# A two-block transformer: the scan's causal mask moves from TensorE products to a 0/1 triangle on the C-B factor

## What is computed

```python
a_cs = jnp.cumsum(a_c, axis=-1)
decay = jnp.exp(segsum(a_c))        # exp(cs[t] - cs[s]) for s <= t, else 0
cb = jnp.einsum("bclgn,bcsgn->bgcls", cm_c, bm_c)
y_diag = jnp.einsum("bgcls,bgrcls,bcsgrp->bclgrp", cb, decay, xs_c)
```

## Time and profile before

| | |
|---|---|
| median of 3 runs | 1653.1 us (1649.43, 1653.1, 1655.61) |
| profiled execution | 1655.45 us, span 1653.8 us |
| PE busy | 1593.0 us, 96% |
| PEld busy | 1541.0 us, 93% |
| POOL busy | 1271.9 us, 77% |
| DVE busy | 925.4 us, 56% |
| ACT busy | 866.3 us, 52% |
| mean DMA rate | 183 GB/s |

### The profile page before, as it was taken

How to read it: one execution, slowest core, us unless ns; L and a number is a source line. 1 busy time by engine, 2 the same in 40 slices (tenths; PEclk the granted TensorE clock), 3 DMA queues, 4 the chain that set the end, 5 groups by cost and what they waited for, 6 DMA issues and landing times.

```text
span 1653.8 us, 33845 instructions
## 1 busy us (share of the span) xinstructions
PE 1593.0 (96%) x13182; PEld 1541.0 (93%) x13182; DVE 925.4 (56%) x1799; ACT 866.3 (52%) x1432; POOL 1271.9 (77%) x948
## 2 busy tenths in 40 slices
PE   7999999999999999999999899999999999999999
PEld 6999988898999999999998899999999998799999
DVE  7767777567646763467677757754442256632200
ACT  3554555554456663465455564545664455655532
POOL 1878967675779999678986767697998786279996
PEclk7999999999999999999999999999999999999999
DMA  8545744446446657455764545654665664146654
GB/s 306 178 146 204 244 165 160 142 166 242 166 141 235 235 200 255 149 156 174 242 207 144 164 155 192 231 178 148 184 190 174 200 202 142 47 152 192 183 188 128
DMA packets 85518, 302.23 MB, mean 183 GB/s; under 512 B 9840, under 2 KB 12528, under 8 KB 85104
## 3 DMA queue, kind: packets, MB, share of 16 engines
q1 hardware_dynamic: 85360, 300.06, 55.3%
HBM read 298.98 MB, written 1.05 MB: 181 GB/s over the span
## 4 chain that ended last, share of the span: by engine, by line
PE 71%; DVE 11%; ACT 5%; DVEq 4%; issue 3%; POOL 2%; DMA 2%; SPq 1%; ACTq 0%; POOLq 0%
PE gemm_bank L1688 63%; ACT w_hi L443 2%; POOL w_lo L425 2%; PE turn_bank L1871 2%; PE turn_bank L1842 2%; DVEq L1337 2%; DVE ada_acc L848 1%; DVE conv L848 1%; DVE h_lo L1383 1%; DVE idx_score L848 1%; DMA ada_first<-in_w_ada 1%; DVE probs L1045 1%; DVEq L1221 1%; PE outp_bank L2078 1%; PE score_bank L1688 1%
## 5 line engine op out<-in xcount | busy, mean ns | idle before, releaser
L425 POOL TENSOR_TENSOR w_lo<-w_raw,w_hi 128x512 fp32r<-128x512 f32 x944 | 1271.7, 1377 | 370.7 <-ACT w_hi L443 357.8
L443 ACT ACTIVATE w_hi<-w_raw 128x1024 fp32r<-128x1024 f32 x472 | 491.7, 1046 | 590.6 <-PE gemm_bank L1688 517.5
L1688 PE MATMUL gemm_bank<-h_hi,w_hi 128*128 128x256 f32 (+1 forms) x2144 | 608.8, 284 | 7.2 <-DVE conv L848 3.7
L1688 PE MATMUL gemm_bank<-h_hi,w_lo 128*128 128x256 f32 (+1 forms) x2144 | 601.2, 280 | 0.0
L1688 PE MATMUL gemm_bank<-h_lo,w_hi 128*128 128x256 f32 (+1 forms) x2144 | 600.8, 280 | 0.0
L1688 PEld LDWEIGHTS gemm_bank<-h_hi,w_hi 128*128 128x128 f32 (+1 forms) x2144 | 403.9, 188 | 16.2 <-issue 7.4
L1688 PEld LDWEIGHTS gemm_bank<-h_lo,w_hi 128*128 128x128 f32 (+1 forms) x2144 | 404.5, 189 | 0.3
L1688 PEld LDWEIGHTS gemm_bank<-h_hi,w_lo 128*128 128x128 f32 (+1 forms) x2144 | 404.0, 188 | 0.2
L848 DVE SCALAR_TENSOR_TENSOR conv<-gemm_bank,params_sb,conv 128x255 f32<-128x255 f32 (+1 forms) x320 | 139.5, 477 | 161.9 <-ACT conv L774 110.7
L1688 PE MATMUL gemm_bank<-w_hi,h_hi 128*128 128x256 f32 (+1 forms) x672 | 193.5, 288 | 2.7 <-DVE h_lo L848 1.5
L1688 PE MATMUL gemm_bank<-w_lo,h_hi 128*128 128x256 f32 (+1 forms) x672 | 188.0, 280 | 0.0
(11 more groups left out here) (310 smaller groups left out, 2165.2 us busy)
## 6 DMA issues: line engine op xcount, KB each, us to landing
w_raw<-in_stream SPq DMA_DIRECT2D x458, 512.0 KB, 3.8
ada_w<-in_w_ada SPq DMA_DIRECT2D x80, 512.0 KB, 4.6
ada_first<-in_w_ada SPq DMA_DIRECT2D x16, 512.0 KB, 12.1
w_raw<-in_stream SPq DMA_DIRECT2D x8, 256.0 KB, 3.1
alibi_sb<-in_alibi SPq DMA_DIRECT2D x1, 1920.0 KB, 7.8
residual<-in_x_t SPq DMA_DIRECT2D x1, 1024.0 KB, 6.7
ada_acc<-in_rows SPq DMA_DIRECT2D x1, 1024.0 KB, 5.1
out_x<-residual SPq DMA_DIRECT2D x4, 256.0 KB, 4.6
```

The lines of the kernel that those rows point to most:

```text
L425: ins = nc.gpsimd.tensor_tensor(w_lo[:, s, e], w_raw[:, s, e], w_hi[:, s, e].bitcast(f32), ALU.subtract)
L443: A(w_hi[:, s, 0:n], w_raw[:, s, 0:n], ACT.Copy).then_inc(hi_ready, 1)
L1688: ins = M(o, a, b, start=first and i == 0, stop=last and i == len(passes) - 1, skip_group_check=True)
```

## The change

The mask is no longer added on PE. A 0/1 triangle `seen_T` (1 where s <= t), made once in the setup, multiplies the diagonal blocks of `CB` as DVE moves them out of PSUM. Since the exponents above the diagonal are now positive and could overflow, ACT first bounds those of the diagonal blocks: it writes relu(cs[s] - cs[t]) with the new column `pos_cs` as bias, and then takes exp of its negative. The block between them (columns 128 to 255) is exponentiated as before. A drain of ACT stands between the Relus and the Exp that reads them. So a head has four ACT instructions and a drain where it had two, and two PE products where it had four.

```diff
-        ident_b = sb("ident_b", [P, P], bf16)
-        maskT_b = sb("maskT_b", [P, P], bf16)
+        seen_T = sb("seen_T", [P, P], bf16)
+        pos_cs = sb("pos_cs", [P, TT, 32])
...
             def decayed_exp(l, h):
                 b, k = S.use(l, S_SSM + h)
                 act.wait_ge(S.full[b], k + 1)
-                A(S.bank[b][:, 0:2 * P], S.bank[b][:, 0:2 * P], ACT.Exp, bias=neg_cs[:, 0, h:h + 1])
-                A(S.bank[b][:, 2 * P:CW], S.bank[b][:, 2 * P:CW], ACT.Exp, bias=neg_cs[:, 1, h:h + 1]).then_inc(decay_done, 1)
+                o = S.bank[b]
+                for c, tt in ((0, 0), (SEQ, 1)):
+                    A(o[:, c:c + P], o[:, c:c + P], ACT.Relu, scale=-1.0, bias=pos_cs[:, tt, h:h + 1])
+                A(o[:, P:SEQ], o[:, P:SEQ], ACT.Exp, bias=neg_cs[:, 0, h:h + 1])
+                act.drain()
+                seen = o[:].rearrange("p (b c) -> p b c", b=2)[:, :, 0:P]
+                A(seen, seen, ACT.Exp, scale=-1.0).then_inc(decay_done, 1)
...
-            V.tensor_copy(ident_b[:], ident)
...
-            V.tensor_copy(maskT_b[:], keep_bias[:, 0:P]).then_inc(set_up, 1)
+            V.tensor_scalar(seen_T[:], keep_bias[:, 0:P], -1.0, None, ALU.is_ge).then_inc(set_up, 1)
...
                 def group_product(g):
                     b, k = S.use(l, S_CB + g)
                     dve.wait_ge(S.full[b], k + 1)
-                    V.tensor_copy(CB[:, g, :], S.bank[b][:, 0:CW]).then_inc(S.read[b], 1)
+                    V.tensor_tensor(CB[:, g, 0:P], S.bank[b][:, 0:P], seen_T[:], ALU.mult)
+                    V.tensor_copy(CB[:, g, P:SEQ], S.bank[b][:, P:SEQ])
+                    V.tensor_tensor(CB[:, g, SEQ:CW], S.bank[b][:, SEQ:CW], seen_T[:], ALU.mult).then_inc(S.read[b], 1)
...
+                        V.tensor_copy(pos_cs[:], T.bank[b][:, 0:64].rearrange("p (t h) -> p t h", t=TT))
                         V.tensor_scalar(neg_cs[:], T.bank[b][:, 0:64].rearrange("p (t h) -> p t h", t=TT), -1.0, None, ALU.mult
...
-                    ins = products([(o[:, 0:SEQ], row, cs_split[:, :]), (o[:, SEQ:CW], row, cs_split[:, P:SEQ]),
-                                    (o[:, 0:P], ident_b[:], maskT_b[:]), (o[:, SEQ:CW], ident_b[:], maskT_b[:])], True, True)
+                    ins = products([(o[:, 0:SEQ], row, cs_split[:, :]), (o[:, SEQ:CW], row, cs_split[:, P:SEQ])], True, True)
```

## The result

The changed kernel takes 1674.35 us (median of 4 runs, 1672.72 to 1677.49), the kernel before on the same chip 1651.26 (4 runs, 1648.99 to 1655.61): ratio on record 1.0123, 95% interval 1.0089 to 1.0156, some 20 us slower (the two medians are 23.1 us apart). The forecast was 1664 us, 11 us slower. The profiled execution took 1677.49 us (span 1675.9), 22.0 more than that of before; the mean granted clock fell from 0.988 to 0.978.

The account below looks back on a forecast made before the run. PE was taken as the bound, 71% of the chain, with ACT and DVE carrying parts of the scans. First layer 5.6 plus second 5.0 made 10.6 us later: profiled 1655.45 to 1666.1, median about 1664, range 1651 to 1674.

Parts of the forecast that it names:

- ScalarE's head: ACT's decay exponentials of one scan head: 0.63 us added to 0.69, bounds 0.45 and 0.80 more.
- No table loads of its own: ACT's Relus in the scan need no table switch; the rival claim was 164 us of loads, chance 1%.
- The three C-B operations: DVE's moves of C-B out of PSUM: three 128-wide take 0.60 us against 0.47, so 0.13 more each time.
- DVE's wait for the exponentials: Sign in the first layer's scan: DVE's wait for ACT grows from 25 to some 36 us.
- The mask products: PE in the scan: a pair is worth 0.13 us; six groups on the chain give back 0.78 a layer.
- rival 1: Scans: PE decides everywhere, ACT's added time hides, mask products are gained: -8.3 + 0.5, 1645 us; chance 8%.
- The second block: Sign: the same stretches stay unchanged in the second block.
- the C-B terms: The C-B factor: two added 0.13 us ahead of PE's wait for the second copy, 0.26 a layer, 0.5 in both.
- The count of heads: Scans: ACT's added time counts 22 times, once for each head whose exponentials are on the chain, less 3.3 us.
- PE's waits for DVE: Sign in the scans: they grow from 7 to about 16 us a layer.
- Rival 3: Scans: longer PE waits cost clock, 1.7 us a fall, two to four more: +3.4 to +6.8, to 1669; chance 13%.
- The bound of 3 us for both layers: Upper limit on the added C-B time, if each 128-wide DVE operation takes 0.42 us.

Follow-up runs that it names:

- experiment 3: Also `pe_only`: kernel before without the mask products on PE, nothing in their place, Tanhs for Exps; 1653.53 us, ratio 0.9999.
- `after_again`: The changed kernel measured once more, unaltered, beside the kernel before; 1673.58 us, ratio 1.0122.
- filler: The changed kernel with unused products on PE ahead of its waits; 1665.3 us, ratio 1.0067.
- `cb_only`: Also experiment 1: kernel before with C-B moved out of PSUM in three 128-wide DVE operations, two masked; mask products and exponentials kept; 1659.71 us, ratio 1.0046.
- `before_delay`: The kernel before with one unused 0.28 us DVE copy ahead of its first C-B copy; 1653.15 us, ratio 1.0007.
- `before_warm`: The kernel before with unused products on PE ahead of its waits; 1656.44 us, ratio 1.0011.
- experiment 9: The same run as `before_delay`: kernel before with one unused 0.28 us DVE copy ahead of its first C-B copy; 1653.15 us, ratio 1.0007.
- number 8: The kernel before with DVE moving C-B out ahead of the top-eight search of the same step; 1648.56 us, ratio 0.9963.
- `after_one_cb`: The changed kernel with C-B moved and masked in one 384-wide DVE operation, using an 8-bit triangle; 1658.02 us, ratio 1.0023.
- `after_all`: The changed kernel with one 384-wide masked C-B operation, C-B ahead of top-eight search, three ScalarE instructions a head and unused PE products; 1657.35 us, ratio 1.0017.

## Why the prediction was right in direction and half in size

**Right.** Direction, and the steps behind it. ScalarE's head: 0.58 us more, for 0.63 forecast. No table loads of its own. The three C-B operations: 0.14 more, for 0.13. DVE's wait for the exponentials: 36.9 us, for "some 36". The mask products: a gain too small to measure, against 8.3 if PE had decided everywhere (experiment 3), so rival 1 is out. The second block lost under 2 us. That 1674.35 lies at the very end of the range, 1674, is luck: that end was worked out with a head of 0.80 more, which measured 0.58, and with two falls of the clock, which were more.

**Right in size, by another route.** The scans were forecast 10.1 us longer (10.6 less the C-B terms); they grew by 8.5 in this run (150.6 + 147.8 against 145.1 + 144.9), by 9.6 in `after_again`. The count of heads was low: the forecast had 22 on the path, the chain of the changed kernel has 26, 13 in each scan. But PE's waits for DVE grew by 4.5 us in the first scan and 4.8 in the second, not by the 9 each that the forecast named. Less the 8.3 us of products that are gone, these waits alone would give 1.0. The clock records of the scans have one fall before and five after, seven in `after_again`; with 1.7 us each that is the rest, 6.8 to 10.2. With filler there was none, and the scans grew by 4.4. That smaller added waits and the falls of the clock together come near the forecast's 10.1 is luck. Waits and clock can't be parted cleanly: a slower PE comes later to its waits and finds them shorter.

**Wrong, the clock.** Rival 3 had the mechanism, its price and 13%, and it was kept as an alternative to the sum. It came on top of it: filler gives back 9 us. This is the term that the sum had at nothing. It was also counted in the scans alone, two to four times 1.7. It came there, in both C-B stages (5.0 us together) and in the second attention, which lost 5.0. In that last place some kernels with the old exponentials have such falls too, in their profiled runs (`cb_only`, `pe_only`, `before_delay`, `before_warm`). In the first attention it is even the other way round, 10.2 us at 1.2 GHz before and 3.4 after. So it is open whether the change is what lowered the clock there.

**Wrong, the C-B factor.** This term of the sum was 0.26 us a layer. It counted the copies ahead of the one that PE waits for, and took every operation between them at its old duration. The running sum stands between them, beside a busy POOL, and grew by 1.1 us because it started on the other side of a POOL instruction (experiments 1 and 9). The measured wait is 1.23 longer a layer, and with the clock the stages lost 8.3 us. The bound of 3 us for both layers was from the C-B operations' own durations, so it didn't hold this. Alone, the C-B part costs 7.6 us (3.6 to 11.6).

**The parts don't add.** Alone they measure +7.6 (C-B), +18.7 (exponentials) and 0 (products), 26 together for 20. The exponentials' part has the widest interval (13 to 24), and the clock and the pace of PE's stream differ from run to run. With the clock loss taken off, the spans are longer than before's by 3 us (C-B), 11 (exponentials) and 9 (all of the change), and 1 shorter (products); the clock loss has grown by 2, 5, 10 and 0. So without the clock the exponentials cost about what their forecast had.

## What to carry to other kernels

Where the profile shows that longer waits of PE cost clock, put that price into the sum instead of keeping it as an alternative, and test it with filler products. Before an instruction is put ahead of others on VectorE, look at which of these run beside a busy GpSimd: a shift of 0.2 us can change another instruction's time by 1 us. Work taken from the busiest engine gains nothing where a chain through two others ends later, and an order change on another of PE's waits (number 8) gained 6 us, where the products on the chain were worth 1.6.

## What the runs showed of the hardware

**The lock between DVE and POOL.** In all 14 profiled runs the running sums of the two layers take either 0.68 us, where they begin 0.06 to 0.09 us ahead of a POOL product (which then takes 1.7), or 1.70 to 1.78, where they begin 0.05 to 0.13 behind its start; nothing lies between. In every such case they end 0.54 us after POOL's product. The second block's running sum does the same: 0.68 in twelve runs, and 1.62 in the two in which it begins 0.21 behind POOL's start, again ending 0.54 after POOL's product.

**Two paces of PE.** At the full clock the 256-column products of a weight stream follow each other in one of two spacings. PE's timeline near the end, the kernel before, then `after_one_cb`:

```profile
1599.75 0.28 PE L1688 MATMUL gemm_bank<-f_lo,w_hi 128*128 128x256 f32 x1
...
1601.16 0.28 PE L1688 MATMUL gemm_bank<-f_lo,w_hi 128*128 128x256 f32 x1
```

```profile
1599.80 0.28 PE L1696 MATMUL gemm_bank<-f_lo,w_hi 128*128 128x256 f32 x1
...
1601.16 0.28 PE L1696 MATMUL gemm_bank<-f_lo,w_hi 128*128 128x256 f32 x1
```

Both are twelve products apart: 1.41 us or 117.5 ns each, and 1.36 us or 113.3 ns. At the end of the trace, from 1550 us on, five of the 14 profiled runs have the faster pace, of kernels with and without the change. But from 1200 to 1250 us only `after_one_cb` and `after_all` have it, at 113.3 ns, and the other twelve all have 117.8; from 50 to 1450 us more than half of the stream of these two is fast, and 11 to 22% of that of the others (twelve spacings in a row with a mean under 115.5 ns count as fast). Two profiles at 1240 us, `after_all`, then `after_again`, again twelve products apart:

```profile
1239.75 0.28 PE L1694 MATMUL gemm_bank<-h_lo,w_hi 128*128 128x256 f32 x1
...
1241.11 0.28 PE L1694 MATMUL gemm_bank<-h_lo,w_hi 128*128 128x256 f32 x1
```

```profile
1239.76 0.28 PE L1695 MATMUL gemm_bank<-h_hi,w_lo 128*128 128x256 f32 x1
...
1241.17 0.28 PE L1695 MATMUL gemm_bank<-h_hi,w_lo 128*128 128x256 f32 x1
```
